# Cached keys in another row order: four successive rows to a partition, and a write with a stride of four behind the transposes

## The reference

```
k_sb  = concat([cache_sb_k[l], new])        # (8, 512 + 16, 6, 64)
z     = einsum('bqhd,bkhd->bhqk', q, k) * 64 ** -0.5
sb:   a = sigmoid(z) * product of sigmoid(-z) over all later keys
fox:  p = softmax(z + decay[k] - decay[q])
dsa:  p = softmax(z where the key is among the 132 best of the indexer)
out   = einsum('bhqk,bkhd->bqhd', a or p, v)
```

## Time and profile before

| | |
|---|---|
| median of 3 runs | 2344.7 us (2344.66 to 2344.75) |
| span of the profiled execution | 2342.9 us (the median lies 1.8 us above it) |
| PE busy | 2308.4 us, 99% of the span |
| DVE, ACT, POOL busy | 1254.6, 566.3, 68.8 us |
| granted TensorE clock | 0.997 |

### The profile page before, as it was taken

One profiled execution on the slowest core, in us unless ns is written; L12 is line 12 of the kernel. 1 busy time (PEld: TensorE's weight loads), 2 busy tenths in 40 slices (PEclk: granted clock), 3 DMA queues, 4 the chain that ended last, 5 costly groups with the idle time before them and its releaser, 6 DMA issues.

```text
span 2342.9 us, 41433 instructions
## 1 busy us (share of the span) xinstructions
PE 2308.4 (99%) x17024; PEld 2060.3 (88%) x17024; DVE 1254.6 (54%) x2700; ACT 566.3 (24%) x1349; POOL 68.8 (3%) x112
## 2 busy tenths in 40 slices
PE   7999999999999999999999999999999999999998
PEld 5999997886688699999999999978866886999998
DVE  5566432634756446565375664426355654666742
ACT  3000013113564231001130010321245642400011
POOL 0000000000022000000000000000000220000000
PEclk9999999999999999999999999999999999999999
DMA  9455234782489453443435533447725984233332
GB/s 335 139 177 176 96 129 153 220 275 88 144 273 345 144 182 114 156 144 99 135 123 178 177 133 115 166 132 239 257 68 169 336 304 148 73 108 109 100 121 77
DMA packets 300509, 390.10 MB, mean 166 GB/s; under 512 B 31005, under 2 KB 251033, under 8 KB 300322
## 3 DMA queue, kind: packets, MB, share of 16 engines
q1 hardware_dynamic: 281090, 336.41, 42.5%
q0 software_dynamic: 11712, 42.18, 5.2%
q10 hardware_dynamic: 7520, 8.87, 1.0%
HBM read 375.30 MB, written 12.12 MB: 165 GB/s over the span
## 4 chain that ended last, share of the span: by engine, by line
PE 95%; DMA 2%; ACT 1%; DVE 1%; issue 1%; SPq 0%; ACTq 0%; DVEq 0%
PE PS L722 31%; PE PS L818 13%; PE PS L1008 7%; PE PS L956 5%; PE PS L1275 4%; PE PS L905 4%; PE PS L978 3%; PE PS L664 3%; PE PS L1174 2%; PE PS L1094 2%; PE PS L866 2%; PE PS L874 2%; PE PS L1307 2%; PE PS L1315 2%; PE PS L1214 2%; PE PS L759 1%
## 5 line engine op out<-in xcount | busy, mean ns | idle before, releaser
L722 PE MATMUL PS<-OT,RING 128*128 128x192 f32 x1280 | 234.2, 326 | 0.0
L722 PE MATMUL PS<-H,RING 128*128 128x192 f32 x1280 | 222.1, 327 | 0.0
L722 PE MATMUL PS<-OT,QR 128*128 128x192 f32 x1280 | 221.1, 326 | 0.0
L722 PEld LDWEIGHTS PS<-OT,RING 128*128 128x128 f32 x1280 | 212.4, 190 | 0.0
L722 PEld LDWEIGHTS PS<-H,RING 128*128 128x128 f32 x1280 | 208.4, 190 | 3.8 <-issue 3.2
L722 PEld LDWEIGHTS PS<-OT,QR 128*128 128x128 f32 x1280 | 210.2, 190 | 0.0
L1419 ACT ACTIVATE QR<-QR 128x384 f32<-128x384 f32 x80 | 41.8, 523 | 533.7 <-DVE QR L2004 533.7
L1008 PE MATMUL PS<-H,RING 128*128 128x384 f32 x480 | 161.1, 490 | 0.0
L1008 PEld LDWEIGHTS PS<-H,RING 128*128 128x128 f32 x480 | 88.9, 190 | 60.6 <-issue 4.4
L722 PE MATMUL PS<-H,QR 128*128 128x192 f32 x640 | 117.1, 326 | 0.0
L1860 DVE TENSOR_TENSOR OT<-OT 128x192 f32<-128x192 f32 x168 | 57.5, 352 | 106.3 <-ACT OT L1390 94.2
(11 more groups left out here) (325 smaller groups left out, 4058.9 us busy)
## 6 DMA issues: line engine op xcount, KB each, us to landing
RING<-ffn_w_in SPq DMA_DIRECT2D x80, 1024.0 KB, 7.2
RING<-w_in SPq DMA_DIRECT2D x64, 768.0 KB, 6.3
QR<-w_ada SPq DMA_DIRECT2D x34, 1024.0 KB, 9.8
BIG<-w_ada SPq DMA_DIRECT2D x34, 1024.0 KB, 10.2
RING<-ffn_w_out SPq DMA_DIRECT2D x32, 768.0 KB, 4.7
RING<-ffn_w_out SPq DMA_DIRECT2D x32, 640.0 KB, 5.4
QR<-cache_sb_v POOLq DMA_DIRECT2D x16, 768.0 KB, 5.2
QKT<-cache_sb_k SPq DMA_DIRECT2D x16, 768.0 KB, 5.9
```

The lines of the kernel that those rows point to most:

```text
L722: mm = pe.matmul(PS[:, bank, GROUP[g]], a[:, k, :], x[:, k, :], start=(k == 0), stop=(k == 3))
```

## The change

A key load gives partition p the rows 4p to 4p+3 of the cache, one piece of 6144 bytes, where it gave it the rows p, 128+p, 256+p and 384+p, four pieces of 1536 bytes. A transpose c then turns the rows c, 4+c, 8+c and so on. The two copies out of PSUM put them back: they read a bank from left to right as before, and write element (c, p) to place 4p+c of `KT`, so that successive written elements lie four numbers (16 bytes) apart. Everything behind `KT` is as it was.

```
-                                 ck[l, b].rearrange("(c p) h d -> p c (h d)", p=P)).then_inc(k_full[n % KBUF], 16)
+                                 ck[l, b].rearrange("(p c) h d -> p c (h d)", p=P)).then_inc(k_full[n % KBUF], 16)
...
+                def by_row(ap):
+
+                    return ap.rearrange("q i (p c) -> q i c p", c=PC)
+
                 def turned_fourth(s):
 
                     act.wait_ge(kt_ready, 2 * (l * NSTEP + s) + 2)
-                    A(KT[s % 2][:, 3, 0:PAST], PS[:, 3, :], ACT.Copy).then_inc(kt_free, 1)
+                    A(by_row(KT[s % 2][:, 3:4, 0:PAST]), PS[:, 3:4, :].rearrange("q i (c p) -> q i c p", c=PC), ACT.Copy).then_inc(kt_free, 1)
 
                 def turned_three(s):
...
-                    A(KT[s % 2][:, 0:3, 0:PAST], PS[:, 0:3, :], ACT.Copy).then_inc(kt_free, 1)
+                    A(by_row(KT[s % 2][:, 0:3, 0:PAST]), PS[:, 0:3, :].rearrange("q i (c p) -> q i c p", c=PC), ACT.Copy).then_inc(kt_free, 1)
```

## The result

The changed kernel takes 2379.29 us (median of 4 runs, 2376.52 to 2380.58), where the kernel before takes 2344.72. The ratio is 1.0143, 95% interval 1.0129 to 1.0158: slower by 34.6 us. The forecast was 2344.0, with a range that ended at 2371.

What follows compares the result with a forecast made beforehand. The prediction took PE, busy for 99% of the span, to bound the kernel, so only its waits could change. It summed 2344.7 - 0.7 for the keys + 0 for the copies = 2344.0 us, range 2342 to 2371.

Steps and rivals of the forecast that it cites:

- The chain of waits: In the sample's attention, `turn_new_probs` waiting on ACT's fourth copy closes first; a longer copy costs only beyond its cover.
- cover: Time between the fourth copy's end and the start of L1245: 1.04 us in SB, 0.97 in FOX, 1.20 in DSA steps.
- the one step without cover: Step 1 of each layer, where PE already waits for the copy, 0.6 us in two times.
- d: Microseconds that both copies out of PSUM gain together in a step; forecast as no more per element.
- the formula: Loss over both layers: 2 x (d + 4(d - 1.04) + 6(d - 0.97) + 5(d - 1.20)), each bracket only where positive.
- the rival: Strided write takes twice as long per element (0.843 ns more), d 1.73 us, priced at +24 us, 2368; chance 0.34.
- The price of the strided write: ACT's two copies into `KT`: 0.843 ns an element before, forecast no more per element with the stride, +0 us.
- the near row: Copies that jump every 16 elements: 384 elements took 483 to 485 ns, against 487 ns without jumps.
- the row of the scan: DVE's scan, 1250 ns for 527 elements, 2.37 ns each: upper bound on the write, d 3.13, loss 68 us, 2413.
- The loads: Key loads in 6144-byte pieces land earlier and remove some of PE's 1.7 us of waits; gain 0.7 us.
- The forecast of the landings: Key loads land sooner than 7.0 us, value loads not sooner than 5.3; L1094's DMA waits shrink.
- the crowding rival: Larger key packets crowd out values and decay rows; about 6 us lost, 2350; chance 0.03.

Runs made afterwards that it cites:

- e6_pe_strided: The change's loads, but TensorE's transposes write PSUM with a stride of four and the copies stay contiguous, correct key order; 2347.2 us, ratio 1.0010.
- e1_loads_only: Only the change's key loads, copies writing contiguously as in the kernel before, so the keys' order differs from the reference's; 2347.6 us, ratio 1.0009.
- e5_read_strided: The change's loads, but the copies read PSUM with a stride of 128 elements and write contiguously, correct key order; 2347.26 us, ratio 1.0007.
- e9_old_loads_mid: e6_pe_strided with key loads 7 to 18 of each layer cut and turned as in the kernel before; 2345.16 us, ratio 1.0002.
- e11_pe_rounds: e6_pe_strided with one of VectorE's selection rounds moved from step 10 to step 6; 2346.34 us, ratio 1.0008.
- e3_stride2: Kernel before, its copies reading a bank as two halves and writing with a stride of two (8 bytes); 2345.65 us, ratio 0.9998.
- e10_rounds_only: Kernel before with one of VectorE's 17 selection rounds moved from step 10 to step 6; 2343.52 us, ratio 0.9994.
- e12_dve_stride4: Kernel before, but VectorE's 24 copies of turned probabilities write with a stride of four; 2346.4 us, ratio 1.0007.
- e2_stride4_only: Kernel before with only the change's stride-four write in both copies, loads as before; 2378.78 us, ratio 1.0140.

## Why the prediction was wrong

**The chain of waits: right.** Which wait closes first, its cover in each kind of step, and the one step without cover were read correctly; with d from the timelines the formula gives the spans of three kernels within 1 us. The waits of `turn_new_probs` alone come to 30.7 us, where the formula gives 30.8. Around them small terms nearly cancel. The transposes for unit 1, ahead of step 0, wait 0.70 us for the long copies of unit 0 in each layer, which the formula leaves out. The last transposes of steps 2 and 5, the SB steps without a gate half, halt for 0.52 us; the rival had priced a full ScalarE there at some tenths. Against it the halts of before (0.19, 0.48, 0.82 and 0.35 us) are gone.

**The price of the strided write: the step that failed.** The prediction said of the cost per element "I take the near row: no more per element". The near rows were copies in runs of 16 elements, and it was noted there that 15 of 16 elements have a neighbour. That was the point: what costs is an element without a neighbour in its 16 bytes, and rows where nearly every element has one say nothing on it. Measured: 1.96 ns in place of 0.84, d = 2.10 us by the durations and 1.96 by the timeline, where the forecast put 0.

**The rival was the right one, undersized.** "Twice as long per element" was given 0.34 and 2368. Its mechanism is what happened, with the wait where it was put. It is 2.3 times, not twice: 1.11 ns more an element in place of 0.84. With d = 1.96 in place of 1.73 the formula gives 30.8 in place of 23.4 us, and what is left to the median's 34.6 fits the lower clock behind the halt of step 1, which no term of the prediction had. With the d of the durations, 2.10, the formula gives 35.2, close to the 34.6; that is luck, since the covers act on 1.96. The range, which ended at 2371, missed 2379.3 because its upper end took the doubling plus 3 us, and the row of the scan, which allowed far more, was left out as without support.

**Which property costs.** The trace after and the runs with strides of 8, 16 and 32 bytes agree with the Trainium skill's "Advanced Engine Details and Errata" (Memory Cachelines), which wants at least two hits on a 16-byte line of SBUF: 0.96, 1.96 and about 1.9 ns an element. It was cited in the prediction beside the rival and should have moved the forecast. The same section says of PSUM that a pattern that isn't contiguous significantly slows matmuls; here the transposes of e6_pe_strided, which write PSUM with a stride of four, stay at 273 ns, and the measurement decides. It tests the writes of float32 transposes only.

**The loads: wrong in sign, small.** Forecast was a gain of 0.7 us. The three kernels with the new loads and copies as short as before, e1_loads_only, e5_read_strided and e6_pe_strided, lie 1.7, 2.1 and 2.0 us above the kernel before that ran beside them; each interval still touches or holds 1. The forecast of the landings was right in direction: key loads land after 6.7 us in e1_loads_only (7.0 before), values after 5.8 (5.3 before), and PE no longer waits for a key load. But those waits were 0.67 us of PE's time in layer 0, not 1.7, and taking them away gained nothing, since VectorE's date in step 11 stood behind them. The byte became cheaper than forecast, too: between 680 and 760 us of e1_loads_only SP's queue takes 39.8/12.09 = 3.29% of the engines' time for each MB, 8% less than the 3.57% of the earlier trace rows.

```profile
q1 hardware_dynamic: 2207, 12.09, 39.8%
```

POOL's queue takes 49.9/13.79 = 3.62% there in place of 3.52%, so over both queues a byte is 2% cheaper. The rule on pieces from 512 bytes up, which the prediction took from the Trainium skill's "DMA: Bandwidth & Descriptors", stands there in the section Specifications, not in the one that it names.

What failed is the date: not the keys but the decay rows had the tightest one, and they were delayed. That was the crowding rival, priced at 6 us and given 0.03. In the change itself this doesn't show: its steps are longer, decay rows land after 6.0 us, and nobody waits for them. That the delayed decay rows lengthen the halts is supported in both layers: in layer 1 by e9_old_loads_mid, where wait and halt go together, in layer 0 by the table above, where the transposes move by what the wait grew. How the larger packets delay the rows was not tried.

## What to carry to other kernels

A float32 write into SBUF with 16 bytes between the starts of successive elements took ScalarE 2.3 times as long an element here, with 8 bytes 1.1 times; if an order must be changed on the way from PE to SBUF, let the copy read PSUM with the stride, or PE write it so, since both were free here. When no row shows an operation, a near row counts only if it shares the property that could cost. And a longer instruction costs what goes beyond its cover: measure the cover in each kind of step, since the sum over the steps then holds within a few per cent. What it doesn't hold is the clock: a halt that gets long can cost its own length and more.

## What the runs showed of the hardware that was not expected

- Writes to SBUF with 16 bytes from element to element end at about 1.07 us for 512 elements on ScalarE and VectorE alike, though contiguous they take 0.59 and 0.68.
- ScalarE's read of PSUM with 512 bytes from element to element took 1452 ns for 1536 elements, as a contiguous one does (1451).
- With key loads in packets of 6144 bytes SP's queue used 8% less DMA time a byte than with packets of 1536, and still the decay rows landed later: after 7.7 to 8.0 us in the median in e1_loads_only, e5_read_strided, e6_pe_strided and e11_pe_rounds, after 6.4 to 7.1 in the kernel before, e3_stride2, e10_rounds_only and e12_dve_stride4.
- The granted clock can fall behind an idle PE of 1.96 to 1.98 us, and need not: it fell to 0.50 for about 3.5 us in both layers of e2_stride4_only and in layer 0 of e1_loads_only, and stayed at 1.00 in both layers of the change's profiled execution and of e5_read_strided. Where it fell in e2_stride4_only, 16 matmuls took 4.50 us in place of 2.83.
